# Two heads' attention weights turned in one PSUM bank and copied once, for steps of up to 256 keys

## What is computed

```python
def forgetting_attention(q, k, v, log_f):        # per head, in blocks of 128 queries
    logits = einsum('bqhd,bkhd->bhqk', qi, k) * scale + decay
    logits = where(causal, logits, NEG_INF)
    p = softmax(logits, axis=-1)
    return einsum('bhqk,bkhd->bqhd', p, v)

# sparse mixer, per block of queries
p_c = masked_softmax(lc, cmp_end <= t)           # at most 31 compressed keys
p_s = masked_softmax(ls, mask_s)                 # selected blocks (all 8 blocks fit)
p_w = masked_softmax(lw, mask_w)                 # window of 512
out = g0 * (p_c @ vc_) + g1 * (p_s @ v_g) + g2 * (p_w @ v_wb)

# merge of the mixers
gates = sigmoid(merge); mixed = sum(gates * branch, axis=2); h = h + mixed @ w_out
```

## Time and profile before

| | |
|---|---|
| median of 3 runs (range) | 2246.1 us (2245.96 to 2246.89) |
| the profiled execution | 2241.13 us, span 2239.8 us, mean granted TensorE clock 0.987 |
| PE busy in the span | 2119.8 us, 95% |
| DVE, ACT, POOL busy | 988.2, 814.8, 227.0 us |
| attention stage of M | from 1606 to 1751 us |
| forgetting heads of layer 0 and 1 | from about 191 to 271 and 850 to 930 us |

### The profile page before, as it was taken

The page is one execution under the profiler, slowest core; times in us unless marked ns, Lnnn a source line. Parts: engine busy times, 40 slices in busy tenths (PEclk is TensorE's granted clock), DMA queues, the critical chain, the costliest instruction groups (busy, mean ns, idle before and its releaser), DMA issues. The chain is left out here.

```text
span 2239.8 us, 25576 instructions
## 1 busy us (share of the span) xinstructions
PE 2119.8 (95%) x10364; PEld 1703.8 (76%) x10364; DVE 988.2 (44%) x1833; ACT 814.8 (36%) x1574; POOL 227.0 (10%) x256
## 2 busy tenths in 40 slices
PE   6899899999998999999999998999798999999997
PEld 5667688888887767688888887878655788888886
DVE  6265453323336375453323336645456444323333
ACT  4145442222234255452222225344256334222322
POOL 3003410000000004310000000000156101000000
PEclk9999999999999999999999999999999999999999
DMA  6521123333322311223233332322411233333321
GB/s 155 110 76 57 57 73 109 97 97 97 103 86 69 108 43 63 67 84 102 92 99 97 96 98 58 98 57 81 104 43 38 67 111 92 94 97 101 94 92 68
DMA packets 273721, 192.10 MB, mean 86 GB/s; under 512 B 22060, under 2 KB 241364, under 8 KB 273604
## 3 DMA queue, kind: packets, MB, share of 16 engines
q1 hardware_dynamic: 268704, 177.76, 27.2%
q0 software_dynamic: 4752, 12.67, 2.4%
q10 hardware_dynamic: 148, 0.04, 0.0%
HBM read 186.21 MB, written 4.23 MB: 85 GB/s over the span
## 5 line engine op out<-in xcount | busy, mean ns | idle before, releaser
L593 PE MATMUL bank<-h_features,weights_hi_lo 128*128 128x512 f32 (+1 forms) x5160 | 1131.4, 380 | 9.5 <-POOL h_features L1915 7.8
L593 PEld LDWEIGHTS bank<-h_features,weights_hi_lo 128*128 128x128 f32 x5160 | 928.7, 189 | 196.0 <-issue 14.8
L927 DVE TENSOR_TENSOR weights_hi_lo<-weights,weights_hi_lo 128x1024 fp32r<-128x1024 f32 (+1 forms) x337 | 402.5, 1198 | 702.2 <-ACT weights_hi_lo L1532 701.7
L1532 ACT ACTIVATE weights_hi_lo<-weights 128x1024 fp32r<-128x1024 f32 (+1 forms) x337 | 341.0, 1016 | 393.1 <-PE bank L635 346.2
L633 PE MATMUL bank<-weights_hi_lo,hidden 128*128 128x512 f32 x528 | 205.4, 389 | 0.0
L634 PE MATMUL bank<-weights_hi_lo,hidden 128*128 128x512 f32 x528 | 205.4, 389 | 0.0
L635 PE MATMUL bank<-weights_hi_lo,hidden 128*128 128x512 f32 x528 | 205.4, 389 | 0.0
L1648 ACT ACTIVATE hidden<-arena 128x512 fp32r<-128x512 f32 x66 | 41.7, 632 | 300.1 <-DVE arena L1078 300.1
L1943 POOL TENSOR_SCALAR arena<-arena,row_stats 128x256 f32<-128x256 f32 (+5 forms) x140 | 126.8, 916 | 170.6 <-DVE row_stats L1004 63.4
L1915 POOL TENSOR_TENSOR h_features<-arena,h_features 128x512 fp32r<-128x512 f32 x24 | 30.7, 1278 | 988.8 <-ACT h_features L1560 988.8
L1078 DVE TENSOR_TENSOR arena<-bank,arena 128x512 f32<-128x512 f32 x66 | 45.6, 692 | 181.3 <-PE bank L593 181.3
(11 more groups left out here) (335 smaller groups left out, 2053.8 us busy)
## 6 DMA issues: line engine op xcount, KB each, us to landing
weights<-in_w_in_dram SPq DMA_DIRECT2D x84, 512.0 KB, 3.9
weights<-in_w_gate_dram SPq DMA_DIRECT2D x66, 512.0 KB, 3.8
weights<-in_w_up_dram SPq DMA_DIRECT2D x66, 512.0 KB, 3.8
weights<-in_w_down_dram SPq DMA_DIRECT2D x60, 512.0 KB, 3.6
weights<-in_w_out_dram SPq DMA_DIRECT2D x24, 512.0 KB, 3.7
bias_rows<-decay_scratch POOLq DMA_DIRECT2D x16, 256.0 KB, 4.0
weights<-in_w_cmp_dram SPq DMA_DIRECT2D x16, 256.0 KB, 4.6
weights<-in_w_down_dram SPq DMA_DIRECT2D x12, 256.0 KB, 2.6
```

Of the source, the lines that this page charges most:

```text
L593: last = e.matmul(out_ap, l, r, start=(j == 0), stop=(j == len(pairs) - 1))
L927: e.tensor_tensor(pair_view(i, 1), raw_view(i), pair_view(i, 0).bitcast(F32), ALU.subtract).then_inc(done, tick(("split", i)))
L1532: e.activation(pair_view(i, 0), raw_view(i), ACT.Copy).then_inc(done, tick(("hi", i)))
```

## The change

A step is now called joint when it is not of kind "diff" and has at most 256 keys. Those are t = 0 and t = 1 of the forgetting heads and of the two wide branches of M, and all cmp steps: 8 in each layer, 32 in M, 48 in all. For a joint step

- PE transposes head 0 into columns 0 to 255 and head 1 into columns 256 to 511 of one bank, so it asks for one bank and not two, and signals once, after head 1;
- one copy takes both heads: by DVE for t = 0 and 2, by ACT for t = 1 and 3. All other steps keep a copy on each engine.

```diff
+            @property
+            def joint(self):
+                return self.kind != "diff" and self.w <= 256
...
+        def turned_views(buffer, t, heads):
+            q = slice(t % 2 * P, t % 2 * P + P)
+            if heads == 2 and t < 2:
+                return [buffer[:, :, 0:t + 1, q]]
+            return [buffer[:, j, 0:t + 1, q] for j in range(heads)]
...
-                return pe.done, pe[*old.name, "turned", j]
+                return pe.done, pe[*old.name, "turned", 0 if old.joint else j]
...
-                return u.t % 2 == 0 if u.kind == "diff" else j == 0
+                return u.t % 2 == 0 if u.kind == "diff" or u.joint else j == 0
+
+            def turned_bank(u, bank):
+                chunks = CHUNKS(u)
+                if u.joint:
+                    return bank[0:chunks[0][1], :].rearrange("p (j b c) -> p j b c", j=2, c=P)[:, :, 0:len(chunks), :]
+                return bank[0:chunks[0][1], 0:len(chunks) * P].rearrange("p (b c) -> p b c", c=P)
...
                 def turn_weights(u, rows):
-                    for j in range(len(u.turned)):
-                        out_ap = bank((*u.name, "turned", j))
+                    for j in range(1 if u.kind == "diff" else 2):
+                        if j == 0 or not u.joint:
+                            out_ap, at = bank((*u.name, "turned", j)), 0
+                        else:
+                            at = 256
...
                         for c, n in CHUNKS(u):
-                            last = e.transpose(out_ap[0:n, c:c + P], rows[j][:, c:c + n], IDENT)
-                        last.then_inc(done, tick((*u.name, "turned", j)))
+                            last = e.transpose(out_ap[0:n, at + c:at + c + P], rows[j][:, c:c + n], IDENT)
+                        if j == 1 or not u.joint:
+                            last.then_inc(done, tick((*u.name, "turned", 0 if u.joint else j)))
...
-                                    e.tensor_copy(u.turned[j], bank[0:rows_n, 0:cols].rearrange("p (b c) -> p b c", c=P)
-                                                  ).then_inc(done, tick((*u.name, "pt", j)))
+                                    e.tensor_copy(u.turned[j], turned_bank(u, bank)).then_inc(done, tick((*u.name, "pt", j)))
...
-                                    e.activation(u.turned[j], bank[0:rows_n, 0:cols].rearrange("p (b c) -> p b c", c=P), ACT.Copy
-                                                 ).then_inc(done, tick((*u.name, "pt", j)))
+                                    e.activation(u.turned[j], turned_bank(u, bank), ACT.Copy).then_inc(done, tick((*u.name, "pt", j)))
```

## The result

| | before | after |
|---|---|---|
| median (range) of 4 runs each, in turn on one chip | 2246.0 us (2245.5 to 2246.9) | 2229.8 us (2226.8 to 2236.1) |
| ratio, 95% interval | | 0.9934 [0.9919, 0.9949] |
| the profiled execution | 2241.1 us, clock 0.987 | 2236.1 us, clock 0.986 |

Its four executions took 2236.1, 2231.9, 2227.8 and 2226.8 us at a mean granted clock of 0.986, 0.988, 0.991 and 0.992. The two profiled executions differ by 5 us, the medians by 16. The gap is the first thing to explain.

A forecast was written before the change was run, and what follows sets the result against it. PE, busy 2119.8 of 2239.8 us, bounds the kernel, so only its waits and low clock could give time. Banks and copies 5.8 plus clock 1.5 made 7.3 us: 2246.1 to 2238.8 us, range 2234.3 to 2243.8.

The forecast's parts named there:

- The sum of banks and copies: M's attention and both layers: shorter bank waits less later values, 2.5 + 0.4 + 0.6 - 0.7 + 0.7 + 2.3 = 5.8 us saved.
- branch tiles 3, 19, 27, 43: Branch fills in M: scores of 256 keys slip ahead of the bank wait, 0.63 us each, 2.5 us saved.
- branch tiles 11 and 35: Branch fills in M with 15-key scores: POOL's scaling limits the gain to at most 0.2 us each, 0.4 us.
- loop step 43: In M, no fill ahead at 39: the wait for DVE's copy before the scores goes, 0.7 us saved.
- gate 15: Gate fill at M's loop step 15: scores slip ahead of the bank wait, 0.6 us saved.
- gates 7, 23, 31: Gate fills in M: no gain; values wait for ACT's longer copy, 0.22 us later each, 0.7 us lost.
- the layers: Head squares in each layer: the second transpose's 1.16 us wait for ACT's L1714 goes, 2.3 us saved in both.
- The clock: M's attention: one stretch at the lower clock level gone, 1.5 us; bounds three gone (-4.5 us) or two more (+3.0).
- A: Rival: waits shrink but the clock doesn't; 2240.3 us, or 2241.8 with one more low stretch; chance 0.20.
- B: Rival: the wait only moves to the transposes; only the layers and loop step 43 gain; 2243.8 us; chance 0.13.
- C: Rival: slower, all longer joint copies show, 7.4 us, and no ring wait shrinks; 2253.5 us; chance 0.04.
- D: Rival: nothing moves, as the scores leading the wait ask for a bank itself not free; 2246.1 us; chance 0.03.

The follow-up runs named there:

- the copies alone: Kernel before, ring unchanged, both heads' copies of a joint step given to one engine as two instructions: 2246.5 us, ratio 1.0004.
- M alone: Against the kernel before, joint banks in M only, layers as before: 2239.3 us, ratio 0.9968.
- early reading: M's fill tiles read at the end of their own loop step: on the kernel before 2234.3 us, ratio 0.9952; on the kernel after 2228.8 us, ratio 0.9927.
- the layers' edit alone: Against the kernel before, joint banks in the two layers' forgetting heads only, M as before: 2240.4 us, ratio 0.9975.

## Why the prediction was right and wrong

**Where the waits are: right.** The order of PE's bank requests decided, as forecast. The waits of L661 for L1795 and L1440 turned into waits of the transposes of 0.5 to 0.9 us, and the ten fell from 11.7 to 6.6 us ("6 or 7" on record). The 1.16 us behind L1714 went in both layers, but "The other head squares and all q/k fills show no PE wait now" was a wrong reading. Each layer has a second wait for L1714 among its differential heads, 0.97 us before and after, since those steps aren't joint:

```profile
172.13 0.44 PE L677 MATMUL bank<-shape_consts,arena 128*128 128x128 f32 x2 [0.97 <-ACT gain_row L1714]
```

No term of the sum rests on it. The copies took 579 and 419 ns (585 and 416). Moving the copies gives nothing and costs little (1.1 us at equal clock, in the kernel with the copies alone).

**The sum of banks and copies: right in kind, somewhat small.** 5.8 us on record; the fill distances show 6.5, the fit 7.4 with an uncertainty of 0.9. Term by term, by the fill distances:
- branch tiles 3, 19, 27, 43: 0.79, 0.6, 0.79 and 0.23 us, 2.4 in all for 2.5;
- branch tiles 11 and 35: 0.05 for the first and not 0.2; the second shares its stretch with loop step 43: 0.96 for 0.2 + 0.7;
- gate 15: 0.64 for 0.6;
- gates 7, 23, 31: 0.12 us of loss each for 0.22. The values wait 1.03, 1.03 and 0.40 us where "about 0.6 us or more" was on record;
- the layers: 1.38 us each for 1.16.

Some 1 us of the 7.4 is in none of these distances, and I can't place it; it is within the uncertainty of the fit.

**The clock: the step that failed.** It reads "I take one stretch gone, 1.5 us, since the idle time of half of the segments falls by half", with three stretches, 4.5 us, as the bound. Measured is 0.0040 of mean clock (within 0.0010), 6.4 us: four times the term and more than the bound. That takes the time below the range, whose best end counted 5.8 us of waits, 4.5 of clock and 1.5 of small terms; the waits' 7.4 for 5.8 is the smaller part of the miss. Three things were weak in the term:
- It counted the stretches of one execution. That one had a clock of 0.987 where 62 executions of the kernel have 0.9853, and its five microseconds below the median were noted in the text and then set aside ("Only differences are formed here"). What the clock can give back depends on the execution, and the median one has some 7 us more at the lower level than the one that was read.
- It looked at M alone. The layers gave 0.0016, as much as M.
- It scaled with idle time, and the runs give no support for that: halving M's waits of 11.7 us gave 0.0017, taking them all away in the kernel before gave 0.0017 too, and taking away the remaining 6.6 us from the kernel after gave nothing that shows (0.9886 and 0.9900 in two kernels, beside 0.9893). But these differences are uncertain by 0.0010 to 0.0015, so a proportional rise isn't excluded either.

The page "TensorE: Matmul & The Clock Gate" of the Trainium skill, section "A second HAM failure mode: psum-queue depth-cycling", tells of a kernel whose short idle spots from cycling through PSUM banks let the clock swing between its levels. The runs here agree in sign: less waiting for banks came with 0.0040 more clock. That page of the Trainium skill gives no size; my own bound of three stretches, a sum of 10.3 us, is nearer to the measured 14.8 than 7.3. I had set it aside for one place where a wait of 1.28 us had no fall behind it, and one place of one execution is too little for that.

**The rivals.** A (no clock) is refuted by 0.0040; B (the wait only moves) by M alone, 4.6 us at equal clock where B has nothing but loop step 43; C (longer copies show) by the copies alone, 1.1 us and not 7.4; D by the seven rows of waits, all shorter.

**What stays open** is which falls of the clock went. In the thirteen profiles at hand the time at the lower level between 1600 and 1760 us (from the granted clock of that window) is 13.6 to 27.3 us in the five with the old waits in M (mean 19.8) and 3.4 to 17 in the eight with joint banks or early reading (mean 8.5). The two groups overlap, but the difference of 11 us, 0.0025 of the span's mean clock, says that a good part of what went lay in M. At the layers' ends it is anything from 0 to 17 us, with the change and without, and the 0.0016 that the layers' edit alone gave has no place yet. One profile of a kernel can't show a shift of 0.004 in the mean. That shorter waits come with a higher clock is shown by the mean clocks: 0.9869 to 0.9900 in the eight kernels whose waits in M, in the layers or in both were cut, 0.9853 to 0.9859 in the three where all were in place. How a wait leads to a fall isn't shown.

## What to carry to other kernels

In a ring of banks count the requests between a tile and the next use of its bank. A tile whose reader comes late is a wait as soon as the ring comes round, and there are two cures, fewer requests or an earlier reader. Try the reader first: here it moved one call on each of two engines and gave 8.6 us in M, where the joint banks gave 4.6. When a change shortens PE's waits in a kernel that PE bounds, reckon the clock apart from the waits, over several executions and over all stages that the change touches, and compare kernels at equal mean clock, or a draw of the clock passes for an effect.

## What the runs showed of the chip

- Executions of one kernel differ by 5 to 14 us, and most of it is the clock: 1.6 us for 0.001 of the mean granted clock, with 1.1 us of scatter around that line over 132 executions of eleven kernels. Before ranged from 2240.9 us at a clock of 0.987 to 2249.8 us at 0.983.
- At the layers' ends the same program at the same place ran at a granted clock of 0.88 and 0.83 in one execution and at 1.00 in another (the windows above).
- A copy from a PSUM bank takes less than twice as long for twice the columns: ACT 368 ns for 256 columns and 579 for 512, DVE 286 for 128 and 419 for 256. Even so one copy in place of two was worth 0.5 us over 48 steps, with an uncertainty of 1.2.
